# Attention's first pair on one core: two weight tiles multiplied block by block, with the norm's squares and sums moved behind them

## The reference

```python
h = rmsnorm(x, norm_gains[layer, 0])
x = x + stick_breaking_mixer(h, sb_w_qkv[j], sb_q_gain[j], sb_k_gain[j], sb_w_o[j])
...
def stick_breaking_mixer(h, w_qkv, q_gain, k_gain, w_o):
    qkv = h @ w_qkv
    q, k, v = jnp.split(qkv, 3, axis=-1)
    q = rmsnorm(q.reshape(bsz, seq, SB_HEADS, SB_HEAD_DIM), q_gain)
    k = rmsnorm(k.reshape(bsz, seq, SB_HEADS, SB_HEAD_DIM), k_gain)
    ...
    o = stick_breaking_attention(q, k, v)
    return o @ w_o
```

## Time and profile before

| | us |
|---|---|
| median of 3 runs | 1837.86 |
| lowest and highest | 1835.81, 1838.56 |
| the profiled execution's own time | 1837.57 |
| its span, first to last instruction | 1835.8 |
| TensorE (PE) busy | 1795.3 (98%) |
| VectorE (DVE) busy | 1028.6 (56%) |
| ScalarE (ACT) busy | 891.4 (49%) |
| GpSimd (POOL) busy | 881.0 (48%) |
| mean granted TensorE clock | 0.994 |

### The profile page before, as it was taken

How to read it: one execution, slowest core, us unless ns; L and a number is a source line. 1 busy time by engine, 2 the same in 40 slices (tenths; PEclk the granted TensorE clock), 3 DMA queues, 4 the chain that set the end, 5 groups by cost and what they waited for, 6 DMA issues and landing times.

```text
span 1835.8 us, 26601 instructions
## 1 busy us (share of the span) xinstructions
PE 1795.3 (98%) x8726; PEld 1411.2 (77%) x8726; DVE 1028.6 (56%) x1663; ACT 891.4 (49%) x1384; POOL 881.0 (48%) x1072
## 2 busy tenths in 40 slices
PE   7999999999999999999899999999999999999999
PEld 5666778888888788888688888888776777776777
DVE  5677667611663487878666413643535565636462
ACT  6767744422343366566444312432456565555562
POOL 3343346655675433434216655766543336543343
PEclk9999999999999999999899999999999999999999
DMA  4211225533443222122045433533221222222212
GB/s 163 67 58 57 63 64 172 168 97 113 158 153 102 81 92 69 59 69 69 23 145 165 138 94 125 180 119 100 81 81 58 70 69 81 81 81 59 79 59 92
DMA packets 49661, 176.85 MB, mean 96 GB/s; under 512 B 5648, under 2 KB 5776, under 8 KB 49568
## 3 DMA queue, kind: packets, MB, share of 16 engines
q1 hardware_dynamic: 42368, 149.44, 26.0%
q10 hardware_dynamic: 7200, 26.22, 4.1%
HBM read 173.54 MB, written 2.10 MB: 96 GB/s over the span
## 4 chain that ended last, share of the span: by engine, by line
PE 81%; DVE 8%; ACT 4%; issue 4%; POOL 2%; DMA 0%; DVEq 0%; ACTq 0%; SPq 0%; POOLq 0%
PE ps_g L244 17%; PE ps_g L251 16%; PE ps_g L248 16%; PE ps_zt L244 6%; PE ps_zt L248 6%; PE ps_zt L251 6%; PE ps_s L1767 1%; POOL w_lo L224 1%; PE ps_o L1222 1%; PE ps_zt L516 1%; PE ps_zt L1818 1%; PE ps_zt L1193 1%; PE ps_o L526 1%; PE ps_s L417 1%; ACT w_hi L216 1%
## 5 line engine op out<-in xcount | busy, mean ns | idle before, releaser
L224 POOL TENSOR_TENSOR w_lo<-raw,w_hi 128x256 fp32r<-128x256 f32 x936 | 770.7, 854 | 787.3 <-ACT w_hi L216 786.2
L216 ACT ACTIVATE w_hi<-raw 128x1024 fp32r<-128x1024 f32 x274 | 288.8, 1054 | 366.4 <-PE ps_zt L251 246.7
L244 PE MATMUL ps_g<-h_hi,w_hi 128*128 128x512 f32 x1240 | 347.1, 410 | 9.9 <-ACT h_hi L294 8.3
L248 PE MATMUL ps_g<-h_lo,w_hi 128*128 128x512 f32 x1240 | 324.0, 391 | 0.6 <-DVE h_lo L304 0.6
L251 PE MATMUL ps_g<-h_hi,w_lo 128*128 128x512 f32 x1240 | 322.6, 391 | 1.0 <-POOL w_lo L224 0.7
L244 PEld LDWEIGHTS ps_g<-h_hi,w_hi 128*128 128x128 f32 x1240 | 224.5, 189 | 76.3 <-issue 23.6
L248 PEld LDWEIGHTS ps_g<-h_lo,w_hi 128*128 128x128 f32 x1240 | 233.4, 188 | 53.2 <-DVE h_lo L304 1.9
L251 PEld LDWEIGHTS ps_g<-h_hi,w_lo 128*128 128x128 f32 x1240 | 233.0, 188 | 51.9 <-POOL w_lo L224 1.9
L361 DVE TENSOR_TENSOR scr<-ps_zt,scr 128x512 f32<-128x512 f32 x32 | 22.1, 692 | 255.3 <-PE ps_zt L251 255.3
L1049 ACT ACTIVATE scr<-ps_g 128x512 f32<-128x512 f32 x64 | 38.3, 599 | 188.3 <-PE ps_g L251 188.3
L244 PE MATMUL ps_zt<-a_hi,w_hi 128*128 128x512 f32 x512 | 128.6, 393 | 0.0
(11 more groups left out here) (214 smaller groups left out, 2388.8 us busy)
## 6 DMA issues: line engine op xcount, KB each, us to landing
raw<-weights SPq DMA_DIRECT2D x274, 512.0 KB, 3.6
scr<-ada_weights ACTq DMA_DIRECT2D x48, 512.0 KB, 4.4
x<-x_tiles SPq DMA_DIRECT2D x8, 256.0 KB, 5.3
y<-x SPq DMA_DIRECT2D x8, 256.0 KB, 2.6
scr<-csil_dram ACTq DMA_DIRECT2D x2, 512.0 KB, 5.3
lvmask<-level_masks SPq DMA_DIRECT2D x1, 960.0 KB, 9.0
mats<-squares SPq DMA_DIRECT2D x1, 448.0 KB, 6.5
vecs<-vectors SPq DMA_DIRECT2D x1, 95.5 KB, 2.0
```

Of the source, the lines that this page charges most:

```text
L216: nc.scalar.activation(w_hi[:, t.rep % 2], raw[:, raw_slot(t)], ACT.Copy).then_inc(whi_ready, 1)
L224: ins = nc.gpsimd.tensor_tensor(w_lo[:, t.rep % 2, ks], raw[:, raw_slot(t), ks], w_hi[:, t.rep % 2, ks].bitcast(F32), ALU.subtract)
L244: nc.tensor.matmul(bank[:], w_hi[:, t.rep % 2, kk], rhs(k)[0], start=(first and n == 0), stop=False)
L248: nc.tensor.matmul(bank[:], w_hi[:, t.rep % 2, kk], rhs(k)[1], start=False, stop=False)
```

## The change

The work of step 0 is written out anew in three functions, `first_pe`, `first_act` and `first_dve`, which `att_pe`, `att_act` and `att_dve` call for the first pair; the old code ahead of step 0 goes away. ACT makes two high parts of x, splits weight tile 1, makes the other six high parts, and only then squares; the eight squares get buffers of their own (`first_xsq`). DVE makes all eight low parts, then the eight sums. TensorE takes tiles 0 and 1 together, for each block high by high of both and weight high by x low of both, into two banks; then the products with low weights of both; then tile 2 into a bank of the scores, with the norm's sum and the lambda product between its first eight and its other sixteen products; then the two heads' sums, into two banks. In step 1 the first half of tile 3 comes ahead of the first scores. SP issues weight tile 1 ahead of the fourth block of x, and weight tile 2 ahead of the square matrices.

```diff
@@ att_z: the bank of tile 2 must have been read
+            if Z_ORDER.index(j) == 1 and a.rep == 0:
+                pe.wait_ge(au_ready, 3)
...
+        first_sq, first_stat = [sq_b, scr[:, 9]], [ps_s[:], ps_o[:]]
+        first_xsq = [scr[:, i] for i in (4, 5, 8, 9, 10, 11, 12, 13)]
...
+        def first_pe(pe):
+            banks = [ps_g[0], ps_g[1], ps_z[2]]
+            def high(t, k):
+                pe.wait_ge(hhi_ready, k + 1)
+                nc.tensor.matmul(banks[t][:], w_hi[:, t % 2, k], h_hi[:, k], start=(k == 0), stop=False)
+            def low(t, k):
+                pe.wait_ge(h_ready, k + 1)
+                nc.tensor.matmul(banks[t][:], w_hi[:, t % 2, k], h_lo[:, k], start=False, stop=False)
+            def rest(t):
+                pe.wait_ge(wlo_ready, t + 1)
+                for k in range(KT):
+                    ins = nc.tensor.matmul(banks[t][:], w_lo[:, t % 2, k], h_hi[:, k], start=False, stop=(k == KT - 1))
+                ins.then_inc(tile_used, 1)
+            for t in range(2):
+                pe.wait_ge(whi_ready, t + 1)
+                high(t, 0)
+                high(t, 1)
+                low(t, 0)
+            for k in range(2, KT):
+                high(0, k)
+                high(1, k)
+                low(0, k - 1)
+                low(1, k - 1)
+            low(0, KT - 1)
+            low(1, KT - 1)
+            rest(0)
+            rest(1)
+            pe.wait_ge(whi_ready, 3)
+            for k in range(KT):
+                high(2, k)
+            norm_pe(pe, 0)
+            nc.tensor.matmul(ps_t[:, 0:4], mats[:, M_ONES], sml[:, 52:56], start=True, stop=True).then_inc(lam_dot, 1)
+            for k in range(KT):
+                low(2, k)
+            rest(2)
+            for n in range(2):
+                pe.wait_ge(att_unit.sq_ready, n + 1)
+                nc.tensor.matmul(first_stat[n], mats[:, M_HEADS], first_sq[n], start=True,
+                                 stop=True).then_inc(att_unit.stat_ready, 1)
...
-            if a: att_z(pe, a, 3)
-            if g: gemm(pe, t, t.rep, h_rhs, H1, True, False, waits, free(0))
+            if a and a.rep: att_z(pe, a, 3)
+            if g: gemm(pe, t, t.rep, h_rhs, H1, True, False, None, free(0))
+            if a and not a.rep: att_z(pe, a, 3)
             if b: att_wt(pe, b, 1)
-            if g: gemm(pe, t, t.rep, h_rhs, H2, False, True, waits)
+            if g: gemm(pe, t, t.rep, h_rhs, H2, False, True)
...
+        def first_act(act):
+            def high(k):
+                act.wait_ge(x_in_sem[k], 16)
+                early_hi(act, 0, k, GAIN[0])
+            def square(k):
+                act.activation(first_xsq[k], x[:, k], ACT.Square).then_inc(xsq_ready, 1)
+            split_hi(act, At(0))
+            high(0)
+            high(1)
+            split_hi(act, At(1))
+            for k in range(2, KT):
+                high(k)
+            for k in range(KT - 2):
+                square(k)
+            split_hi(act, At(2))
+            square(KT - 2)
+            square(KT - 1)
+            split_hi(act, At(3))
+            rstd_act(act, 0)
+            for n, src in enumerate((qn[0], kn[0])):
+                act.wait_ge(au_ready, n + 1)
+                act.activation(first_sq[n], src, ACT.Square).then_inc(att_unit.sq_ready, 1)
+            act.wait_ge(lam_dot, 1)
+            act.activation(sml[:, 56:60], ps_t[:, 0:4], ACT.Exp).then_inc(csil_act, 1)
+            for n in range(2):
+                act.wait_ge(att_unit.stat_ready, n + 1)
+                act.wait_ge(qk_ready, n)
+                act.activation(rstd_b, first_stat[n], ACT.Ln, bias=small[:, 0:1],
+                               scale=1.0 / DH).then_inc(att_unit.ln_done, 1)
+                act.wait_ge(att_unit.ln_done, n + 1)
+                act.activation(rstd_b, rstd_b, ACT.Exp, scale=-0.5).then_inc(att_unit.rstd_ready, 1)
...
+        def first_dve(dve):
+            for k in range(KT):
+                early_lo(dve, 0, k, GAIN[0])
+            for k in range(KT):
+                dve.wait_ge(xsq_ready, k + 1)
+                dve.wait_ge(acc_ready, k)
+                nc.vector.tensor_tensor(acc[:], acc[:], first_xsq[k], ALU.add).then_inc(acc_ready, 1)
+            dve.wait_ge(mats_in_sem, 16)
+            clear_acc(dve, 0)
...
+            att_u_dve(dve, At(0), 0, qn[0])
+            att_u_dve(dve, At(0), 1, kn[0])
+            dve.wait_ge(csil_act, 4)
...
+            att_qk_dve(dve, At(0), 0, qn[0], vec("qg"))
+            att_qk_dve(dve, At(0), 1, kn[0], small[:, 1:2])
...
             for k in range(KT):
+                if k == 3:
+                    weights_in(1)
                 sp.dma_start(x[:, k], x_in[k]).then_inc(x_in_sem[k], 16)
+            weights_in(2)
             sp.dma_start(mats[:], mats_in.rearrange("p (m f) -> p m f", f=P)).then_inc(mats_in_sem, 16)
-            weights_in(1)
-            weights_in(2)
```

More of the change, by code:

```diff
@@ L723, in att_drain_dve @@
             att_olo_dve(dve, a)
+        def first_pe(pe):
[37 more added lines that the diff above has]
+                                 stop=True).then_inc(att_unit.stat_ready, 1)
         def att_pe(pe, g, a, b):
+            if g and g.rep == 0:
+                first_pe(pe)
+                return
             if a and not g:
@@ L732, in free @@
             def free(i):
-                return (au_ready, t.of(1, i - 1)) if t.rep + i >= 2 else None
-            waits = h_waits(0) if g and g.rep == 0 else None
-            if a: att_z(pe, a, 3)
-            if g: gemm(pe, t, t.rep, h_rhs, H1, True, False, waits, free(0))
+                return au_ready, t.of(1, i - 1)
+            if a and a.rep: att_z(pe, a, 3)
+            if g: gemm(pe, t, t.rep, h_rhs, H1, True, False, None, free(0))
+            if a and not a.rep: att_z(pe, a, 3)
             if b: att_wt(pe, b, 1)
-            if g: gemm(pe, t, t.rep, h_rhs, H2, False, True, waits)
+            if g: gemm(pe, t, t.rep, h_rhs, H2, False, True)
             if a: att_z(pe, a, 2)
             if b: att_pv(pe, b)
[L742 to L747, removed]
+            if g: gemm(pe, t + 1, t.rep + 1, h_rhs, H1, True, False, None, free(1))
             if a: att_wt(pe, a, 3)
@@ L791, in att_ohi_act @@
             act.activation(a_hi0[:, b.v], ps_o[:], ACT.Copy).then_inc(ohi_ready, 1)
+        def first_act(act):
[29 more added lines that the diff above has]
+                act.activation(rstd_b, rstd_b, ACT.Exp, scale=-0.5).then_inc(att_unit.rstd_ready, 1)
         def att_act(act, g, a, b):
+            if g and g.rep == 0:
+                first_act(act)
+                return
             if a and not g:
@@ L812, in att_act @@
             if g:
[L813 to L816, removed]
                 act.wait_ge(au_ready, t.of(1, 1))
@@ L874, in att_u_dve @@
                 dve.wait_ge(att_turn.turned, g.v)
-            ins = nc.vector.tensor_tensor(dst, ps_g[t.rep % 2][:], rstd_x, ALU.mult)
-            ins.then_inc(au_ready, 1)
+            bank = ps_z[2] if g.rep == 0 and i == 2 else ps_g[t.rep % 2][:]
+            nc.vector.tensor_tensor(dst, bank, rstd_x, ALU.mult).then_inc(au_ready, 1)
         def att_qk_dve(dve, g, k, dst, gain):
@@ L881, in att_qk_dve @@
             nc.vector.scalar_tensor_tensor(dst, dst, gain, rstd_b, ALU.mult, ALU.mult).then_inc(qk_ready, 1)
+        def first_dve(dve):
[7 more added lines that the diff above has]
+            clear_acc(dve, 0)
+            dve.wait_ge(csil_act, 3)
+            nc.vector.tensor_tensor(csil, vecs[:, VC["c"]:VC["c"] + KT], small[:, 16:24], ALU.mult).then_inc(csil_dve, 1)
+            att_u_dve(dve, At(0), 0, qn[0])
+            att_u_dve(dve, At(0), 1, kn[0])
+            dve.wait_ge(csil_act, 4)
+            for l in range(2):
+                nc.vector.tensor_scalar(sml[:, 60:61], sml[:, 56 + 2 * l:57 + 2 * l], LAM_INIT[l], None,
+                                        ALU.add).then_inc(lam_ready, 1)
+                dve.wait_ge(lam_ready, 2 * l + 1)
+                nc.vector.tensor_tensor(sml[:, 48 + l:49 + l], sml[:, 57 + 2 * l:58 + 2 * l], sml[:, 60:61],
+                                        ALU.subtract).then_inc(lam_ready, 1)
+                dve.wait_ge(lam_ready, 2 * l + 2)
+            att_qk_dve(dve, At(0), 0, qn[0], vec("qg"))
+            att_qk_dve(dve, At(0), 1, kn[0], small[:, 1:2])
         def att_dve(dve, g, a, b):
+            if g and g.rep == 0:
+                first_dve(dve)
+                return
             if a and not g:
@@ L2156, in _ @@
             prologue_act(act)
[L2157 to L2163, removed]
             pipelined(act, att_act, PAIRS)
@@ L2200, in _ @@
             dve.wait_ge(acc_zero, 1)
[L2201 to L2216, removed]
             pipelined(dve, att_dve, PAIRS)
```

## The result

The changed kernel takes 1840.02 us (median of 20 runs, 1837.30 to 1841.42), the kernel before 1836.67 (20 runs, 1834.52 to 1838.56). The forecast was 1839.8, range 1836.2 to 1842.6, "same".

A forecast was written before the change was run, and what follows sets the result against it. TensorE, busy 98%, was taken as the bound, except where it idles or runs at its lower clock. First scores 0.8 later plus 1.5 for idle and clock gave 2.3 on 1837.57, written as 1839.8; range 1836.2 to 1842.6, "same".

The forecast's parts named there:

- the two places: First scores, forecast 0.8 us later, and TensorE's idle ahead of tile 4's low weights, forecast to add 1.5.
- Landing of the second weights: At the start, weight tile 1, issued behind three x tiles, was to land at 8.8 us, its split ending at 9.9.
- the rival of late weights: Second weight tile lands at 10.4 to 11.0 instead of 8.8, delaying the 29 matmuls; 1842.1 with 2.2 late; chance 0.16.
- Rise of the clock: During the first two tiles, TensorE leaves its low clock at 13.7 to 16.8 us; the middle was taken.
- T: End of the first two tiles' 29 matmuls, forecast 19.0 us, between 18.35 and 19.75 by when the clock rises.
- Sum of squares: Ahead of the norm in tile 2, DVE's last sum ends at 25.0 us beside POOL, so TensorE waits 0.5.
- the row that I used: Profile row giving a DVE sum 1.21 us while POOL forms low weights, chosen over the exclusive-port rule's up to 1.6.
- From there on: From norm's sum through the heads' sums to first scores; the serial chain from heads' sum takes 5.4, scores at 35.05.
- Idle time and clock: TensorE idles about 2.7 us ahead of tile 4's low weights, then slow matmuls; 1.5 added, bounds 0 and 1.7.
- The half tile: Half of tile 3 (2.73 us) ahead of first scores is no gain; ACT, DVE and POOL set scores to transposes.
- the first rival: Clock stays up despite the 2.7 idle, so only T counts: 1837.4 to 1839.1, middle 1838.4; chance 0.22.

The follow-up runs named there:

- the run with the filled idle time: Changed kernel with eleven matmuls of no use put ahead of tile 4's low-weight products in step 1; 1838.02 us, ratio 1.0007 to the kernel before.

## Why the prediction was right

The direction, the class and the two places were right, and the time lies 0.2 from the forecast. The shift itself was undersized: 2.3 forecast, against 3.27 of the two profiled executions and 3.35 of the medians. That the number agrees so well is luck: the forecast started from an execution of 1837.57, 0.9 above the median of 20, and the shift was 1.0 short, so two errors cancel.

Step by step. **Landing of the second weights:** 8.8 forecast, 9.47 measured; the rival of late weights had this mechanism, with 10.4 to 11.0. The 29 products began at 10.58 and not at 9.95. **Rise of the clock:** I took the middle between 13.7 and 16.8; in the profile it came at the late end. T is 20.11 and not 19.0. By the prediction's own sum a rise at 16.8 alone gives 19.75, so about 0.75 of the 1.1 is the late rise and 0.36 the late weights. T is the term that was mis-sized. **Sum of squares:** TensorE waited 0.20 for it, not 0.5, since two sums beside POOL took 1.96 and not 2.42. The Trainium skill, "SBUF — State Buffer", section "Who interferes with whom", has a DVE instruction with two SBUF inputs and a GpSimd one that reads SBUF take whole turns at an exclusive port. The trace is further from that than the row that I used, at 0.98 a sum against 0.68 alone. **From there on:** 4.83 from the norm's sum to the heads' sum (4.65 forecast), 5.53 to the scores (5.4). The scores were 2.03 later, not 0.8. **Idle time and clock:** 2.60 idle (2.7 forecast, though its terms, 10.1 less 7.2, give 2.9) and 1.51 lost behind it (3.54 - 2.03; 1.5 forecast), which the run with the filled idle time confirms at 1.54. **The half tile:** that it is no gain by itself was right for the time (1840.31 with the scores first again, 1840.02 without), but not for the reason given. ACT, DVE and POOL do not set the stretch alone; with slow products behind the scores, TensorE's second scores set it. One other sum is off: the first rival's 1837.4 comes out as 1837.7 from its own T of 18.35.

Where the gain went that one might look for: the two tiles together no longer go at the pace of ACT's squares and DVE's sums, but their 29 products start only with the second weights and run into the lower clock, which before the change had lain in a tile that waited for ACT and DVE (the 0.30 at 18.15); and the half tile saved ahead of the scores comes back as idle time in front of the same low weights.

## What to carry to other kernels

Work that is moved ahead of a wait on the critical chain takes cover away behind it: look for the next wait that it had filled, and move what that wait is for (here the split of tile 4) along with it. Where TensorE runs dry, price the slow products behind the idle time too, and try a few matmuls of no use in it. Price the start of a program at the pace its matmuls show there.

## What the runs showed that was not expected

The same first stage saw the clock rise at different times: its high products ended from 18.68 to 20.11 in four profiles, two of them, 19.45 and 19.86, on one chip. So up to 1.4 us at the start can differ between executions of the same program; whether the chip has a part in it was not tried.

Behind an idle time the clock did not always fall, either. The prediction had 1.68 of idle time as harmless from one profile. In the twelve profiles of these runs that same wait was followed by slow products three times; with the second weight tile one block earlier, for example, the row of two reads 1.07, where nine profiles read 0.73:

```profile
265.60 1.07 PE L251 MATMUL ps_g<-a_hi,w_lo 128*128 128x512 f32 x2 [1.68 <-POOL w_lo L224]
```

Idle times of 2.08 to 2.23, near 1583 and ahead of the second transposes, were followed by slow products in 11 of 15 cases, and those from 2.32 up in every case. (In the earlier trace rows the row at 1316.28 itself still reads 1.17; the slow ones stand right behind it, 1.88 at 1317.28 and 1.90 at 1318.95.) So for waits of 1.7 to 2.2 us the price of a fall comes in some executions and not in others.

From 890 to 920 us, where no edit reaches, the granted clock was 0.77 in the profiles of the kernel before, of the changed one and of two more, and 0.89 in the other eight. That such differences make up the spread of 2 to 5 us between runs of one kernel is likely, but was not tried.
